# The seven block products in 26 up tiles of the MLP, with GpSimd forming the first of a pair's three weight sums instead of VectorE

## The chip, the cores and the metric

The kernel runs on one NeuronCore of a Trainium2 chip. The metric is the time of one execution on the device, in microseconds (us). Engines: TensorE (PE; PEld is its weight load), VectorE (DVE), ScalarE (ACT), GpSimd (POOL) and SyncE (SP), which here only issues transfers.

## The reference, cut to what matters

A Mamba-2 layer, shared keys and values, a differential attention layer, and then a second block: a mixer layer and an MLP, 512 tokens by 1024 features in fp32. The change touches the MLP, which is computed after 16 further tokens have been put in front (they are dropped again at the end):

```python
u = _rmsnorm(h, mlp_norm_g[l])
h = h + jnp.square(jax.nn.relu(u @ w_up[l])) @ w_down[l]   # w_up 1024 x 4096, w_down 4096 x 1024
h = _rmsnorm(h, final_norm_g)
```

## The kernel before

**Layout.** Activations are kept transposed: features on the 128 partitions, tokens along the free axis. An "up tile" is 128 of the 4096 columns of w_up for all 512 tokens: 8 blocks of 128x128 weights (a unit), each multiplied with 128 features x 512 tokens. Each fp32 product is made of three fp32r matmuls, high x high, high x low and low x high part, so a tile has 24 matmuls of 512 columns (`tile_of`, L522, matmul L543). The high part of a unit's weights is a copy by ScalarE (`hi`, L1143), the low part a subtraction by VectorE (`lo`, L1677: w_lo = w_raw - w_hi). w_raw, w_hi and w_lo have two slots each, a unit being loaded 512 KB at a time by SP's queue (`load`, L363), as soon as the low part of the unit before the last has been formed.

**The MLP.** 16 up tiles, 16 units of w_down over the features these gave (added to h), 16 more up tiles, and a last stage with the rest of w_down that puts out tokens on partitions (`down`, L1105). After an up tile VectorE takes relu(x) times the RMS norm's factor rt of each token from PSUM into ft (L2437), squares it (L2442) and subtracts (L2444), ScalarE squares it into b_hi (L1621); b_hi and b_lo are the high and low part for w_down. The norm's factor comes out of the first tiles' time: ScalarE's root, VectorE's reciprocal (L2430), a spread by TensorE, a copy into rt (L1614). In the last stage VectorE turns h into osb block by block (L2476) between the units.

**What sets the order.** Nothing is scheduled by a planner: each engine has its own list of instructions, written out by hand, and goes through it in order; waits on counting semaphores (raw, hi_ready, lo_ready, unit_done, acc_read, fh_ready, fl_ready) tie the lists together. An engine whose next instruction waits runs nothing of what stands behind it. GpSimd has nothing to do in the MLP but one transfer near its end (L515). Earlier in the kernel it makes two additions a group: L493 and L487 (one input there is a broadcast).

## Time and profile before

| | |
|---|---|
| median of 3 runs | 1231.15 us (1231.12 to 1231.21) |
| the profiled execution | span 1229.6 us, first to last instruction |
| TensorE busy | 1218.7 us (99%), 6181 matmuls |
| VectorE, ScalarE, GpSimd busy | 867.6 (71%), 596.6 (49%), 52.0 us (4%) |
| MLP's up and down tiles | 865.41 to 1133.65 us of the span |
| data moved | 115.24 MB, mean 94 GB/s |

The profile has this one execution; the median is over runs without it. A matmul's duration includes its way through the array, so durations of successive ones overlap; what a matmul costs is the distance between two starts. A group of rows has a busy time and the mean duration of one instruction; a timeline row has the start and the duration. What an engine idles ahead of an instruction stands in square brackets, with what ended it.

### The profile page before, as it was taken

Reading aid. Unit: us, or ns where it says so; the run is one execution under the profiler, and the core shown is the slowest. Engines: PE = TensorE matmul, PEld = TensorE weight load, DVE = VectorE, ACT = ScalarE, POOL = GpSimd, SP = SyncE. Lnnn points to the kernel's source line nnn. Section 1 sums busy time; section 2 is a strip of 40 time slices with the busy share of each in tenths; the row PEclk is TensorE's granted clock in tenths of the full one; section 3 lists DMA queues with packets and bytes.
Section 4 is the critical chain, followed back from the end, with each engine's and each line's share of the span. In section 5 each row is a group of like instructions: output and inputs, shape, how many; then the busy total and the mean of one; then the engine's idle time right before and its main releaser. Section 6 shows DMA issues by size and latency. Waiting matters only on the chain.

```text
span 1229.6 us, 17316 instructions
## 1 busy us (share of the span) xinstructions
PE 1218.7 (99%) x6181; PEld 990.3 (81%) x6181; DVE 867.6 (71%) x1342; ACT 596.6 (49%) x955; POOL 52.0 (4%) x46
## 2 busy tenths in 40 slices
PE   8999999999999999999999999999999999999997
PEld 6788888888888887878787899758888888888886
DVE  5888889888965366767777789997555332555676
ACT  6666755675653255565555553774323121222222
POOL 1010111111110000000000000000000000000000
PEclk9999999999999999999999999999999999999999
DMA  6433333333324322222222222124233323232322
GB/s 171 139 97 110 97 95 106 112 91 98 108 63 145 103 86 69 77 79 68 68 68 82 73 87 86 34 74 115 86 98 89 102 86 102 86 102 87 119 86 102
DMA packets 182606, 115.24 MB, mean 94 GB/s; under 512 B 3601, under 2 KB 175921, under 8 KB 181537
## 3 DMA queue, kind: packets, MB, share of 16 engines
q1 hardware_dynamic: 180672, 104.02, 29.1%
q0 software_dynamic: 1888, 10.62, 2.5%
q8 instruction: 28, 0.46, 0.2%
q14 instruction: 18, 0.14, 0.0%
HBM read 112.46 MB, written 2.16 MB: 93 GB/s over the span
## 4 chain that ended last, share of the span: by engine, by line
PE 96%; DVE 2%; DMA 1%; issue 0%; ACT 0%; SPq 0%; ACTq 0%
PE psum L543 66%; PE psum L1105 6%; PE psum L811 4%; PE psum L743 4%; PE psum L917 3%; PE psum L972 2%; PE psum L780 2%; PE psum L798 1%; PE psum L647 1%; PE psum L655 1%; PE psum L638 1%; PE psum L792 1%; PE psum L629 1%; PE psum L623 1%; PE psum L986 1%; PE psum L1056 1%
## 5 line engine op out<-in xcount | busy, mean ns | idle before, releaser
L1143 ACT ACTIVATE w_hi<-w_raw 128x1024 fp32r<-128x1024 f32 x184 | 194.4, 1057 | 412.2 <-PE psum L543 334.1
L1677 DVE TENSOR_TENSOR w_lo<-w_raw,w_hi 128x1024 fp32r<-128x1024 f32 x184 | 224.9, 1222 | 131.9 <-ACT w_hi L1143 131.5
L543 PE MATMUL psum<-a_hi,w_hi 128*128 128x512 f32 (+1 forms) x864 | 315.1, 380 | 0.2
L543 PE MATMUL psum<-a_lo,w_hi 128*128 128x512 f32 (+1 forms) x864 | 310.9, 375 | 0.0
L543 PE MATMUL psum<-a_hi,w_lo 128*128 128x512 f32 (+1 forms) x864 | 309.6, 373 | 0.0
L543 PEld LDWEIGHTS psum<-a_hi,w_hi 128*128 128x128 f32 x864 | 157.4, 188 | 34.2 <-issue 3.9
L543 PEld LDWEIGHTS psum<-a_hi,w_lo 128*128 128x128 f32 x864 | 157.2, 188 | 30.2
L543 PEld LDWEIGHTS psum<-a_lo,w_hi 128*128 128x128 f32 x864 | 157.0, 188 | 28.8
L543 PE MATMUL psum<-b_hi,w_hi 128*128 128x512 f32 x376 | 149.9, 399 | 0.0
L543 PE MATMUL psum<-b_lo,w_hi 128*128 128x512 f32 x376 | 148.6, 395 | 0.0
L543 PE MATMUL psum<-b_hi,w_lo 128*128 128x512 f32 x376 | 148.0, 394 | 0.0
L543 PEld LDWEIGHTS psum<-b_hi,w_hi 128*128 128x128 f32 x376 | 70.7, 188 | 21.8 <-issue 5.8
L543 PEld LDWEIGHTS psum<-b_hi,w_lo 128*128 128x128 f32 x376 | 70.7, 188 | 16.1
L543 PEld LDWEIGHTS psum<-b_lo,w_hi 128*128 128x128 f32 x376 | 70.6, 188 | 15.9 <-issue 0.2
L2437 DVE SCALAR_TENSOR_TENSOR arena<-psum,rt 128x512 f32<-128x512 f32 x32 | 22.1, 692 | 54.4 <-PE psum L543 52.5
L1105 PE MATMUL psum<-w_lo,b_hi 128*128 128x512 f32 x128 | 50.5, 394 | 0.0
L1105 PE MATMUL psum<-w_hi,b_lo 128*128 128x512 f32 x128 | 50.4, 394 | 0.0
L1105 PE MATMUL psum<-w_hi,b_hi 128*128 128x512 f32 x128 | 50.4, 394 | 0.0
L2228 DVE SCALAR_TENSOR_TENSOR arena<-arena,par 128x512 f32<-128x512 f32 x60 | 43.4, 750 | 0.6
L2476 DVE STREAM_TRANSPOSE arena<-h 32x128 f32<-32x128 f32 (+1 forms) x128 | 36.6, 286 | 3.9
L811 PE MATMUL psum<-w_hi,a_hi 128*128 128x256 f32 x128 | 36.8, 287 | 0.0
L811 PE MATMUL psum<-w_lo,a_hi 128*128 128x256 f32 x128 | 36.0, 281 | 0.0
(331 smaller groups left out, 1819.4 us busy)
## 6 DMA issues: line engine op xcount, KB each, us to landing
w_raw<-a_w_in SPq DMA_DIRECT2D x48, 512.0 KB, 3.8
w_raw<-w_up SPq DMA_DIRECT2D x32, 512.0 KB, 4.0
w_raw<-w_down SPq DMA_DIRECT2D x32, 512.0 KB, 3.8
arena<-acs POOLq DMA_DIRECT2D x8, 1024.0 KB, 5.0
w_raw<-a_w_out SPq DMA_DIRECT2D x16, 512.0 KB, 3.7
w_raw<-w_kv SPq DMA_DIRECT2D x16, 512.0 KB, 3.6
w_raw<-b_w_in SPq DMA_DIRECT2D x16, 512.0 KB, 3.8
w_raw<-w_in SPq DMA_DIRECT2D x14, 512.0 KB, 3.7
```

Of the source, the lines that this page charges most:

```text
L543: ins = mm(out, wv[:, u.par, k, :], xv[:, k0 + k, c0:c0 + cn], start=(first and begin and i == 0 and n == 0), stop=(last and end and i == ...
L743: ins = mm(bank((1, 0, 2, 3)[j]), wv[:, u.par, n, :], xv[:, k * KT + n, 0:SEQ], start=(k == 0 and n == 0 and i == 0), stop=(k == 1 and n = ...
L780: ins = mm(bank(2 + 2 * (q % 2) + i)[:, 0:P * (q + 1)], aq[64 * i:64 * i + 64, s.par, P * q:P * q + P], ak[64 * i:64 * i + 64, s.par, 0:P ...
L811: ins = mm(out, xv[:, 4 * part + k, P * c:P * c + P], value_block(wv, u)[:, k, :], start=(part == 0 and c % 2 == 0 and k == 0 and n == 0), ...
L917: ins = mm(acc(m), wv[:, u.par, 2 * k + j, :], xv[:, x, 0:SEQ], start=(k == 0 and n == 0), stop=(k == 3 and n == 2), skip_group_check=True)
L972: ins = mm(bank(2 * m.par), w_raw[:, u.par, k, :], h[:, k, META:T2], start=(k == 0), stop=(k == KT - 1), skip_group_check=True)
L1105: ins = mm(bank(4 * (1 - f) + i), b[:, k0 + k, P * i:P * i + P], w[:, k, :], start=(k0 + k == 0 and w is wh and b is b_hi and (f, i) != (1 ...
L1143: ac(w_hi[:, u.par, :, :], w_raw[:, u.par, :, :], ACT.Copy).then_inc(S["hi_ready"], 1)
L1677: tt(w_lo[:, u.par, :, :], w_raw[:, u.par, :, :], f32(w_hi[:, u.par, :, :]), ALU.subtract).then_inc(S["lo_ready"], 1)
L2228: ins = stt(dwo[:, j, :], src, par[:, at:at + 1], dwo[:, j, :], ALU.mult, ALU.add)
L2437: stt(ft, acc(m + (M_MLP + 24 * half)), 0.0, rt[:, 0:SEQ], ALU.max, ALU.mult).then_inc(S["acc_read"], 1)
L2476: own(nc.vector.transpose(osb[32 * q:32 * q + 32, 0:n, P * m + 32 * i:P * m + 32 * i + 32], h[32 * i:32 * i + 32, m, META:META + P * n].re ...
```

## The change

The 6 first up tiles stay as they are but for their tail: relu and square are now ScalarE's, without the factor rt. The factor is applied after w_down instead (its square on the sums, by VectorE; in the last stage with a per-token scalar, for which the residual is brought in scaled where it needs to be). The other 26 tiles go in 13 pairs, 5 in the first half and 8 in the second. A pair's product is seen as 2x2 blocks, [2 halves of the 1024 features] x [2 tiles] for the weights and [2 halves of the features] x [2 halves of the tokens] for the activations, and formed with seven block products instead of eight (Winograd's form of Strassen's scheme). Each block product has 4 blocks of 128 features, three matmuls each, and 256 tokens: 12 matmuls of 256 columns.

It needs sums on both sides. On the activations' side four (t1 to t4) are formed once, during the six plain tiles, by VectorE and ScalarE, high and low parts too. On the weights' side three for each pair: PR (two block sums in one addition, 1024 elements per partition), Q = one of PR's plus a block, U = Q plus a block (512 each). GpSimd forms PR (`pair_sum`), VectorE Q and U. High parts (A, D, PR, Q, U) are ScalarE's, low parts VectorE's. On the products' side ScalarE copies M1, U2 and M5 out of PSUM (`keep`), VectorE adds C22 and C12, ScalarE takes the relus of all four quarters and squares. Weights of a pair are loaded in one transfer of 1 MB (`load_pair`), into one of two places, once the low part D of the pair before the last is there; the place of even pairs lies over t3 and t4's fp32 form. The order of TensorE is M1, M4 of the pair before, M6, M2, M5, M7, M3.

Not shown: reading helpers that turn a name and a pair number into a semaphore and a count; `slot_free` (a high part waits for the product that last read its place); `keep`, `first_row`, `second_row`, `right_columns`, `squares_high`, `squares` (one ScalarE instruction each: copies of M1, U2, M5; relu of C11, of C21, of C12 and C22; the square into b_hi, the square in place); `pair_lo`, `b_pair`, `t_low` (one subtraction each); the list of both engines during the plain tiles; the last stage's added scalars.

```diff
+UP_PLAIN = 6
+U_DOWN = U_MLP + UP_PLAIN
+U_LAST = U_DOWN + 16
+U_END = U_LAST + 16
+PAIRS = (5, 8)
+PAIR0 = (0, 5)
...
+            def load_pair(q):
+                i = q - PAIR0[q >= PAIR0[1]]
+                src = t["w_up_2"].rearrange("(k p) m -> p k m", p=P)
+                c0 = P * (UP_PLAIN + 2 * q if q < PAIR0[1] else 16 + 2 * i)
+                sp.dma_start(pair_raw[i % 2].rearrange("p k a m -> p k (a m)"), src[:, :, c0:c0 + 2 * P]
+                             ).then_inc(on_raw(q)[0], 16)
+            def load_pairs(half, first, second):
+                for i in range(PAIRS[half]):
+                    q = PAIR0[half] + i
+                    if i < 2:
+                        sp.wait_ge(*(first, second)[i])
+                    else:
+                        sp.wait_ge(*on_lo("D", q - 2))
+                    load_pair(q)
+            for m in range(UP_PLAIN):
+                load(Lin(U_MLP + m), t["w_up_2"], 0, Lin(m * P))
+            load_pairs(0, (S["t_sum"], USED + T_DONE), (S["lo_ready"], U_DOWN))
...
+            load_pairs(1, on_lo("D", 4), (S["lo_ready"], U_LAST))
...
+            def pair_sum(q):
+                v = raw_of(q)
+                pool.wait_ge(*on_raw(q))
+                if q:
+                    pool.wait_ge(*on_lo("PR", q - 1))
+                else:
+                    pool.wait_ge(S["t_sum"], USED + T_DONE)
+                nc.gpsimd.tensor_tensor(sum_pr, v[:, 0], v[:, :, :, 1, :].rearrange("p h k m -> p k h m"), ALU.add
+                                        ).then_inc(S["w_sum"], 1)
+            for q in range(PAIR0[1] + PAIRS[1]):
+                pair_sum(q)
...
+            def product(name, q, wh, wl, xh, xl, out, first):
+                for k in range(4):
+                    for i, (wv, xv) in enumerate(((wh, xh), (wh, xl), (wl, xh))):
+                        ins = mm(out, wv[:, k, :], xv[:, k, :], start=(first and k == 0 and i == 0),
+                                 stop=(k == 3 and i == 2), skip_group_check=True)
+                ins.then_inc(on_pe(name, q)[0], 1)
...
+            def m4(q):
+                pe.wait_ge(*on_added("C22", q))
+                pe.wait_ge(*on_lo("D", q))
+                product("M4", q, s_hi["D"], s_lo["D"], t_hi[3], t_lo[3], pair_a(q), False)
+            def pairs(half):
+                for i in range(PAIRS[half]):
+                    q = PAIR0[half] + i
+                    m1(q)
+                    if i:
+                        m4(q - 1)
+                    if q == 0:
+                        pe.wait_ge(S["t_sum"], USED + T_DONE)
+                    pe.wait_ge(*on_kept("M1", q))
+                    product("M6", q, s_hi["Q"], s_lo["Q"], t_hi[1], t_lo[1], pair_a(q), False)
+                    product("M2", q, s_hi["A"][:, 1], s_lo["A"][:, 1], x_block(a_hi, 1, 0), x_block(a_lo, 1, 0),
+                            bank(1)[:, 0:256], False)
+                    pe.wait_ge(*on_lo("PR", q))
+                    if i:
+                        pe.wait_ge(*on_added("C12", q - 1))
+                    else:
+                        pe.wait_ge(S["acc_read"], M_DOWN + 8 * half)
+                    if q == 0:
+                        pe.wait_ge(S["t_sum"], USED + T_DONE + 1)
+                    product("M5", q, s_hi["PR"][:, :, 1], s_lo["PR"][:, :, 1], t_hi[0], t_lo[0], bank(0)[:, 0:256], True)
+                    pe.wait_ge(*on_kept("U2", q))
+                    product("M7", q, s_hi["PR"][:, :, 0], s_lo["PR"][:, :, 0], t_hi[2], t_lo[2], pair_a(q), False)
+                    pe.wait_ge(*on_lo("U", q))
+                    pe.wait_ge(*on_kept("M5", q))
+                    product("M3", q, s_hi["U"], s_lo["U"], x_block(a_hi, 1, 1), x_block(a_lo, 1, 1),
+                            bank(0)[:, 0:256], False)
+                m4(q)
...
+            def up(m):
+                act.wait_ge(S["unit_done"], U_MLP + m + 1)
+                if m >= 2:
+                    act.wait_ge(S["fl_ready"], m - 1)
+                v = fts[0][:, m % 2, :]
+                ac(v, acc(Lin(M_MLP + m)), ACT.Relu).then_inc(S["acc_read"], 1)
+                act.wait_ge(S["acc_read"], M_MLP + m + 1)
+                ac(b_hi[:, m, 0:SEQ], v, ACT.Square)
+                ac(v, v, ACT.Square).then_inc(S["fh_ready"], 1)
...
+            def pair_hi(name, q):
+                slot_free(name, q)
+                if name in ("A", "D"):
+                    act.wait_ge(*on_raw(q))
+                    src = raw_of(q)[:, :, :, 0, :] if name == "A" else raw_of(q)[:, 1, :, 1, :]
+                else:
+                    act.wait_ge(*on_sum(name, q))
+                    src = {"PR": sum_pr, "Q": sum_q, "U": sum_u}[name]
+                ac(s_hi[name], src, ACT.Copy).then_inc(on_hi(name, q)[0], 1)
...
+            def pairs(half):
+                n, q0 = PAIRS[half], PAIR0[half]
+                for i in range(n):
+                    q = q0 + i
+                    pair_hi("U", q)
+                    keep("M1", q)
+                    if i:
+                        second_row(q - 1)
+                    pair_hi("D", q)
+                    if i:
+                        right_columns(q - 1)
+                    keep("U2", q)
+                    if i < n - 1:
+                        pair_hi("Q", q + 1)
+                    if i:
+                        squares_high(q - 1)
+                    if i < n - 1:
+                        pair_hi("A", q + 1)
+                    keep("M5", q)
+                    if i:
+                        squares(q - 1)
+                    first_row(q)
+                    if i < n - 1:
+                        pair_hi("PR", q + 1)
+                u = (U_DOWN, U_LAST)[half]
+                act.wait_ge(*on_pe("M7", q))
+                hi(Lin(u))
+                right_columns(q)
+                second_row(q)
+                hi(Lin(u + 1))
+                squares_high(q)
+                squares(q)
+            ac(gfm[:, :], par[:, C_MLP:C_MLP + KT], ACT.Copy, scale=-1.0).then_inc(S["t_hi"], 1)
+            act.wait_ge(S["t_sum"], USED + 1)
+            for k in range(4):
+                ins = ac(t_f32[0][:, k, :], t_f32[0][:, k, :], ACT.Copy, scale=par[:, C_MLP + k:C_MLP + k + 1])
+            ins.then_inc(S["t_hi"], 1)
...
+            pair_hi("Q", 0)
+            pair_hi("A", 0)
+            up(4)
+            pair_hi("PR", 0)
+            act.wait_ge(S["half_read"], USED + 1)
+            ac(t_hi[0], t_f32[0], ACT.Copy).then_inc(S["t_hi"], 1)
+            up(5)
+            pairs(0)
...
+            def pair_sums(q, names):
+                v = raw_of(q)
+                for name in names:
+                    if q:
+                        dve.wait_ge(*on_lo(name, q - 1))
+                    if name == "Q":
+                        dve.wait_ge(*on_sum("PR", q))
+                        tt(sum_q, sum_pr[:, :, 1, :], v[:, 0, :, 0, :], ALU.add).then_inc(S["w_sum"], 1)
+                    else:
+                        dve.wait_ge(*on_sum("Q", q))
+                        tt(sum_u, sum_q, v[:, 1, :, 0, :], ALU.add).then_inc(S["w_sum"], 1)
...
+            def add_c22(q):
+                dve.wait_ge(*on_pe("M7", q))
+                dve.wait_ge(*on_kept("M5", q))
+                stt(fts[q % 2][:, 1, 256:512], bank(2 + q % 2)[:, 0:256], -1.0, keep_m5, ALU.mult, ALU.subtract
+                    ).then_inc(S["w_added"], 1)
+            def add_c12(q):
+                dve.wait_ge(*on_pe("M3", q))
+                tt(fts[q % 2][:, 0, 256:512], bank(0)[:, 0:256], keep_u2, ALU.add).then_inc(S["w_added"], 1)
...
+            def pairs(half):
+                n, q0 = PAIRS[half], PAIR0[half]
+                for i in range(n):
+                    q = q0 + i
+                    pair_lo("U", q)
+                    pair_lo("D", q)
+                    if i < n - 1:
+                        pair_sums(q + 1, ("Q", "U"))
+                        pair_lo("Q", q + 1)
+                        pair_lo("A", q + 1)
+                    if i:
+                        b_pair(q - 1)
+                    add_c22(q)
+                    if i < n - 1:
+                        pair_lo("PR", q + 1)
+                    add_c12(q)
+                u = (U_DOWN, U_LAST)[half]
+                lo(Lin(u))
+                lo(Lin(u + 1))
+                b_pair(q)
...
+            for m in range(8):
+                u = U_DOWN + 2 * m
+                if m < 7:
+                    lo(Lin(u + 2))
+                else:
+                    pair_sums(5, ("Q", "U"))
+                dve.wait_ge(S["unit_done"], u + 2)
+                part = fts[0][:, 0, :]
+                tt(part, acc(Lin(M_DOWN + m)), rt[:, 0:SEQ], ALU.mult).then_inc(S["acc_read"], 1)
+                dve.wait_ge(S["acc_read"], M_DOWN + m + 1)
+                own.mark(tt(h[:, m, META:T2], h[:, m, META:T2], part, ALU.add))
+                if m < 7:
+                    lo(Lin(u + 3))
+                else:
+                    pair_lo("Q", 5)
+                    pair_lo("A", 5)
+                    pair_lo("PR", 5)
+            pairs(1)
```

## Rows read from the trace of the kernel before

**Rows 1.** The page's chain of work that ended last, shares of the span by engine.

```profile
PE 96%; DVE 2%; DMA 1%; issue 0%; ACT 0%; SPq 0%; ACTq 0%
```

**Rows 2.** Busy time by stage: us from:to, length, then each engine's busy time (instructions), clock, DMA share, GB/s.

```profile
1038.00:1133.80 95.80, 95.80 (x415) 77.69 (x414) 51.32 (x63) 25.84 (x32) 0.00 (x0) 1.00 0.33 98
```

**Rows 3.** Timeline of TensorE: start us, duration us, engine line op out<-in.

```profile
900.13 0.39 PE L543 MATMUL psum<-a_hi,w_hi 128*128 128x512 f32 x1
...
955.73 0.39 PE L543 MATMUL psum<-b_hi,w_hi 128*128 128x512 f32 x1
...
1044.69 0.39 PE L543 MATMUL psum<-a_hi,w_hi 128*128 128x512 f32 x1
...
1133.65 0.39 PE L1105 MATMUL psum<-w_hi,b_hi 128*128 128x512 f32 x1
```

**Rows 4.** Timeline of TensorE in the attention layer, matmuls of 256 columns.

```profile
442.76 0.28 PE L811 MATMUL psum<-w_hi,a_lo 128*128 128x256 f32 x1
...
445.01 0.28 PE L811 MATMUL psum<-w_lo,a_hi 128*128 128x256 f32 x1
```

**Rows 5.** Groups by shape, whole kernel: busy us, mean ns | idle before, released by.

```profile
L1143 ACT ACTIVATE w_hi<-w_raw 128x1024 fp32r<-128x1024 f32 x184 | 194.4, 1057 | 412.2 <-PE psum L543 334.1 <-PE psum L1105 56.6 <-PE psum L743 13.4
...
L1388 ACT ACTIVATE arena<-psum 128x384 f32<-128x384 f32 x16 | 7.0, 487 | 30.4 <-PE psum L792 30.4
...
L1398 ACT ACTIVATE arena<-psum 128x128 f32<-128x128 f32 x32 | 8.4, 278 | 22.5 <-PE psum L798 22.5
...
L1677 DVE TENSOR_TENSOR w_lo<-w_raw,w_hi 128x1024 fp32r<-128x1024 f32 x184 | 224.9, 1222 | 131.9 <-ACT w_hi L1143 131.5
...
L1858 DVE TENSOR_TENSOR arena<-arena,psum 128x256 f32<-128x256 f32 x16 | 6.7, 421 | 0.6
```

**Rows 6.** Timeline of ScalarE and VectorE behind an up tile.

```profile
883.65 1.06 ACT L1143 ACTIVATE w_hi<-w_raw 128x1024 fp32r<-128x1024 f32 x1 [3.92 <-PE psum L543]
...
884.62 0.62 ACT L1621 ACTIVATE b_hi<-arena 128x512 f32 x1
...
884.75 1.23 DVE L1677 TENSOR_TENSOR w_lo<-w_raw,w_hi 128x1024 fp32r<-128x1024 f32 x1 [0.40 <-ACT w_hi L1143]
...
885.89 0.69 DVE L2442 TENSOR_TENSOR arena<-arena 128x512 f32<-128x512 f32 x1
```

**Rows 7.** Group of GpSimd's 2048-wide addition, one input broadcast.

```profile
L487 POOL TENSOR_TENSOR arena<-arena,gacs 128x2048 f32<-128x2048 f32 x7 | 25.6, 3651 | 0.6
```

**Rows 8.** Timeline around GpSimd's 512-wide additions, the first and the last of eight.

```profile
82.68 1.22 DVE L1677 TENSOR_TENSOR w_lo<-w_raw,w_hi 128x1024 fp32r<-128x1024 f32 x1
...
83.34 1.71 POOL L493 TENSOR_TENSOR arena<-arena 128x512 f32<-128x512 f32 x1 [13.46 <-ACT arena L1244]
...
84.00 1.61 DVE L1778 SCALAR_TENSOR_TENSOR arena<-arena,gconv 128x512 f32<-128x512 f32 x1
...
85.64 0.75 DVE L1779 SCALAR_TENSOR_TENSOR arena<-arena,gconv 128x512 f32<-128x512 f32 x1
...
362.75 1.30 POOL L493 TENSOR_TENSOR arena<-arena 128x512 f32<-128x512 f32 x1 [21.75 <-ACT arena L1244]
```

**Rows 9.** Timeline of VectorE during GpSimd's 2048-wide addition of 90.81 to 94.46.

```profile
92.42 0.69 DVE L1771 TENSOR_TENSOR arena<-psum,rt 128x512 f32<-128x512 f32 x1 [0.18 <-PE psum L543]
```

**Rows 10.** Timeline of the start of the MLP.

```profile
868.45 0.75 DVE L2416 SCALAR_TENSOR_TENSOR a_lo<-h,par,a_hi  x1
...
871.78 0.47 PE L543 MATMUL psum<-a_hi,w_hi 128*128 128x512 f32 x1
...
873.89 0.18 DVE L2430 RECIPROCAL stat<-stat 128x4 f32<-128x4 f32 x1 [0.35 <-ACT stat L1153]
```

**Rows 11.** Transfers by issue: queue, count, KB each, median us from issue to landing.

```profile
w_raw<-w_up SPq DMA_DIRECT2D x32, 512.0 KB, 4.0
...
w_raw<-b_w_out SPq DMA_DIRECT2D x8, 512.0 KB, 3.4
...
arena<-acs POOLq DMA_DIRECT2D x8, 1024.0 KB, 5.0
```

## What the change does to the time: the prediction

> **What bounds the kernel now.** I read the chain of work that ended last first: 96% of the span is TensorE [rows 1], so time goes only where its matmuls stop or become fewer. The stage table shows the same for the second half's up tiles: TensorE is busy for all of 95.80 us, VectorE for 51.32, ScalarE for 25.84 [rows 2]. The beat of TensorE is read from starts, not from durations, which overlap: 384 matmuls of 512 columns lie between 955.73 and 1044.69 and again between 1044.69 and 1133.65 [rows 3], 0.2317 us each, so a plain up tile (24 of them) takes 5.56 us and two take 11.12. For half as many columns, the 19 starts from 442.76 to 445.01 give 0.118 us [rows 4] although each has its own weight load: a narrow matmul costs half, and the weight loads stay hidden. The clock is at full speed all through this stage [rows 2].
>
> **What is removed: one product in eight.** A pair of tiles was 48 wide matmuls, 11.12 us. It becomes 7 x 4 x 3 = 84 narrow ones, 84 x 0.117 = 9.84 us, 1.41 a product. Were TensorE never to wait, 13 pairs would give 13 x 1.28 = 16.6 us.
>
> **What is added: work on the other engines.** Per pair ScalarE gets two 1024-wide and three 512-wide high parts, five 256-wide copies or Relus, one 512-wide Relu and two 1024-wide squares. A 1024-wide one takes 1.06 us [rows 5], but in a row the next one starts 0.97 after it, and a 512-wide one counts 0.53 (0.62 less that overlap) [rows 6]. For 256 elements out of PSUM I take 0.38, between 0.28 for 128 and 0.49 for 384 [rows 5], 0.29 in a row. Sum: 4 x 0.97 + 4 x 0.53 + 5 x 0.29 = 7.5 us. VectorE gets three 1024-wide (1.23 [rows 5], 1.15 in a row [rows 6]), five 512-wide (0.69, 0.61 in a row) and two 256-wide ones (0.42 [rows 5], 0.34 in a row): 7.2 us. Both fit into 9.84. So it is not the load that decides, it is the order.
>
> **The price of GpSimd's sum.** No row has this add: 1024 elements from two SBUF inputs. The nearest: 512 elements took 1.30 us with VectorE quiet [rows 8], 2048 with one broadcast input 3.65 [rows 7]. The line through these gives 2.08, doubling the first 2.60. I take 2.35, the middle; both ends are kept.
> The Trainium skill (GPSIMD Engine Reference, § 3.1) has a two-input add of 2048 fp32 elements at 4497 ns; half of it, 2.25, is an estimate that would make the period below 10.7 and the kernel 1229.5 us; no run here shows that size. Its § 4.1 sends elementwise adds to VectorE, which speaks against this change.
> The second part of the price is in VectorE's rows: a two-input operation that started at 84.00, while GpSimd's add of 83.34 to 85.05 ran, took 1.61 us [rows 8] where the same ones take 0.75 otherwise; it ended 0.56 after GpSimd did. GpSimd in turn took 1.71 instead of 1.30, with a VectorE subtraction in flight at its start [rows 8]. An operation with one input in PSUM kept its 0.69 beside GpSimd's 2048-wide add [rows 9]. So one of the two with two SBUF inputs waits for the other, and all of VectorE's sums and low parts have two.
>
> **The chain that sets a pair's time.** After pair_lo("PR") VectorE has add_c12, lo U, lo D, then sum Q, which waits for GpSimd's sum, which waits for that same lo PR. From its end: handoff 0.08, GpSimd 2.35; lo U, held until then, ends 0.50 later (0.69 less the 0.19 by which the held one was shorter); lo D 0.61; sum Q 0.61; handoff 0.04 (884.71 to 884.75 [rows 6]); on ScalarE hi Q 0.53, squares_high 0.97, hi A 0.97, keep M5 0.29, squares 1.06; handoff 0.04; on VectorE b_pair 1.15, add_c22 0.34, the next lo PR 1.22. Sum 10.76 us. If lo U gets in ahead of GpSimd, it is 10.87. I take 10.8 a pair. TensorE, with 9.84, would wait some 0.9 us, before M3, which needs keep M5 (its end at 7.0 of the period, while M7 is done at 6.3). M4 then comes at once, since C22 is there when M1 has run. The other cycle (M4, second_row, hi D, lo D) has hi D 1 us before lo D can start, so it doesn't count.
>
> **The start of the MLP.** VectorE is free at 869.2 [rows 10] and now has, before its reciprocal: the first difference 1.2, a wait for ScalarE's four scalings 1.6, four 256-wide steps 1.6, lo 1.2. The reciprocal ends at about 875.0 instead of 874.07 [rows 10]; TensorE has done half of tile 1 (started at 871.78 [rows 10]) at 874.6, so it waits 0.4 us and the plain tiles end at 900.5 instead of 900.13 [rows 3].
>
> **The first pairs.** load_pair(0) waits for t_low(4), since its buffer holds t3 and t4. ScalarE and VectorE work through their lists behind tile 2's end, so t_low(4) ends at about 889.1. A load is now 1 MB. Those of 512 KB took 3.4 to 4.0 us, the lower number being that of b_w_out's, which reads runs of 1 KB as these do; 1024 KB of acs took 5.0 [rows 11]. Bounds 5.0 and 8.0 (twice 4.0); I take 5.0, since the one row with this size has it: landed 894.2. Then GpSimd 2.4 and sum Q 0.7: 897.4. ScalarE follows with hi Q 0.53, hi A 0.97, up(4) 1.75, hi PR 0.97, t_hi 0.97, up(5) 1.75, hi U 0.53, keep M1 0.38: 905.3. M1(0) runs at 900.5, M6(0) at 905.4: TensorE waits 3.4 us there. M3(0) starts at 911.05, lo PR(1) ends at 913.6. Three periods, 32.4, bring 946.0 for lo PR(4). The last pair has no next one to prepare: M4(3) ends 0.6 after that, five products 7.05, M4(4) waits 0.3 for squares(3), b_pair(3) and add_c22(4), then 1.4: 955.5. Before, the down tiles started at 955.73 [rows 3]: -0.2 us for the first half, where 5 x 1.28 = 6.4 were on offer.
>
> **The down tiles** keep their 88.96 us. VectorE has two operations more a tile instead of one (0.7 + 0.7 where it had 0.7, beside two low parts of 1.23, in 11.1 us of TensorE); that is covered. Without the cover it would cost 8 x 0.7.
>
> **The second pairs.** VectorE's last h addition stands ahead of lo Q(5) and lo A(5), and waits for all down tiles. From the end of down: 0.2 + 0.69 + 0.04 + 0.69 + 0.04, lo Q 0.61, lo A 1.22 = 3.5 us in which TensorE stands; M6(5) waits 0.7 more for keep M1(5). lo PR(6) ends 13.9 after the end of down. Six periods 64.8, the last pair 9.55 as above: 88.25 instead of 88.96, -0.7 us.
>
> **The last stage** keeps its matmuls; the residual additions are one operation each as before, one tiny one and a 512-wide one more: +0.1.
>
> **Sum.** -0.2 - 0.7 + 0.1 = -0.8 us. The profiled execution has a span of 1229.6 us and the median of the runs is 1231.15, so 1.55 us lie around the span: 1228.8 + 1.55 = 1230.4 us. This kernel's measurement can tell about 0.2%, 2.5 us, from no change.
>
> **Rivals.**
> (a) GpSimd's sum doesn't hold VectorE (other buffers, other moment). Then lo U and lo D run beside it, sum Q ends 3.12 after lo PR instead of 4.15, the chain is 9.73 and TensorE's 9.84 bounds. Nine periods by 0.9: 1222.3 us. Against it: the 1.61 [rows 8]. Chance 0.15.
> (b) Slower: GpSimd's sum is longer than my bound, or has to wait for VectorE's next operation also. Each us goes into the chain nine times and into both starts. From 2.65 on the kernel is slower than before by anything one can measure; at 3.0 the period is 11.4, the time 1230.4 + 9 x 0.6 = 1236. Chance 0.2.
> (c) Slower: the loads. load_pair(q) leaves after lo D(q-2), 3.5 us after lo PR; the sum needs it 10.8 + 0.1 after that lo PR, so 7.3 us may pass. At the bound of 8.0 the first load is 3.0 us later, once, and each period 0.7 longer: 1230.4 + 3.0 + 9 x 0.7 = 1239.7; from 7.6 on the kernel is measurably slower. For it: a load moves twice the bytes; against it: the 5.0 [rows 11]. Chance 0.1.
> My forecast has 0.55, with a range of its own from 1228 (sum at 2.08) to 1233 (sum at 2.60 and load at 5.6).
>
> **How the numbers follow.** Faster by over 0.2% (below 1228.7): (a) and 0.13 of the forecast's 0.55, 0.28. Slower (over 1233.6): (b) and (c) without their mild part, 0.27, and 0.06 for starts longer than worked out, 0.33. Between: 0.39. The range takes in (a) and most of (b) and (c): 1222.5 to 1238.
>
> **What would show it.** In the profile after: a distance of 10.8 us from one M3 to the next, not 9.84 or 11.1; TensorE idle about 0.9 us ahead of each M3, released by ScalarE's copy into keep_m5; 13 GpSimd adds of 2.1 to 2.6 us, and VectorE's subtraction for U with 2 us instead of 0.69; gaps of 3.4 us after M1(0) and of 3.5 us ahead of M1(5). The prediction is wrong if TensorE waits ahead of another product, if GpSimd waits for a DMA, or if the period is TensorE's own.

## The result, and the profile after

| | before | after |
|---|---|---|
| median (lowest to highest) of 15 runs | 1231.11 us (1230.72 to 1232.94) | 1236.88 us (1233.16 to 1239.13) |
| profiled execution, span | 1229.6 us | 1235.6 us |
| TensorE busy | 1218.7 us | 1212.1 us |

The ratio is 1.0041, 95% interval 1.0033 to 1.0049: the change makes the kernel 5.8 us slower. The forecast was 1230.4 us, no change that could be measured. The time lies in the range, but on the slow side, which had a chance of 0.33, and it got there by a mechanism that none of the rivals named: the range held by luck. The 15 runs don't scatter at random. The two with a mean granted clock of 0.999 took 1233.16 and 1233.27 us, those with 0.994 or 0.995 took 1236.5 to 1237.3. A mean of 0.999 leaves room for at most 3.7 us at half clock in the whole run, its end included (estimate: 2 x 0.0015 x 1231.6), where the profiled run has 10.2 us at the two starts that are described below.

The page of the kernel after: engines, then of the picture in 40 slices the rows of TensorE and its clock, the chain of work that ended last, and the new load.

```profile
PE 1212.1 (98%) x6649; PEld 1007.6 (82%) x6649; DVE 912.7 (74%) x1386; ACT 668.2 (54%) x1093; POOL 84.3 (7%) x59
...
PE   9999999999999999999999999999989999999997
...
PEclk9999999999999999999999999999989999999999
...
PE 85%; DVE 8%; ACT 3%; issue 2%; DMA 2%; POOL 0%; SPq 0%; ACTq 0%; DVEq 0%
...
arena<-w_up SPq DMA_DIRECT2D x7, 1024.0 KB, 5.3
```

TensorE's part of the chain fell from 96% [rows 1] to 85%, VectorE's rose from 2% to 8%. The single 8 in each row of the picture is the slice in which the first pairs start, and it is in the clock's row too: TensorE not only waited there, it ran slower afterwards. The stage table of after shows it (from:to, length, then busy time of TensorE, its weight loads, VectorE, ScalarE and GpSimd, granted clock, DMA share, GB/s):

```profile
905.00:909.00 4.00, 3.15 (x15) 3.19 (x16) 4.00 (x4) 1.47 (x4) 1.91 (x1) 0.50 0.00 0
912.00:959.00 47.00, 45.24 (x379) 44.69 (x378) 35.98 (x40) 32.06 (x55) 7.20 (x3) 1.00 0.25 78
959.40:1048.40 89.00, 89.00 (x385) 71.93 (x384) 32.10 (x35) 20.83 (x21) 2.40 (x1) 1.00 0.36 106
...
1052.00:1055.00 3.00, 2.89 (x12) 2.59 (x12) 1.58 (x2) 0.08 (x1) 1.88 (x1) 0.50 0.00 0
1056.00:1139.00 83.00, 78.93 (x657) 77.85 (x657) 67.45 (x74) 56.63 (x96) 14.40 (x6) 1.00 0.28 90
```

The clock was at half (1.2 GHz instead of 2.4) behind the start of the first pairs and behind the start of the second, and full in between; before had 1.00 in its up and down tiles, as in [rows 2]. The records put the two stretches at 904.99, for 6.83 us, and at 1051.76, for 3.41 us. The matmuls show the same (TensorE's timeline of after at the two starts):

```profile
902.60 0.28 PE L1196 MATMUL psum<-a_hi,pair_lo 128*128 128x256 f32 x1
905.85 0.55 PE L1196 MATMUL psum<-t_hi,q_hi 128*128 128x256 f32 x1 [2.97 <-ACT psum L1841]
906.19 0.42 PE L1196 MATMUL psum<-t_lo,q_hi 128*128 128x256 f32 x1
...
935.06 0.35 PE L1196 MATMUL psum<-a_hi,w_hi 128*128 128x256 f32 x1 [0.75 <-ACT arena L1841]
...
945.98 0.36 PE L1196 MATMUL psum<-a_hi,w_hi 128*128 128x256 f32 x1 [0.76 <-ACT arena L1841]
...
1048.13 0.40 PE L663 MATMUL psum<-b_hi,w_lo 128*128 128x512 f32 x1
1051.99 0.55 PE L1196 MATMUL psum<-a_hi,pair_hi 128*128 128x256 f32 x1 [3.46 <-DVE pair_lo L2760]
1052.34 0.41 PE L1196 MATMUL psum<-a_lo,pair_hi 128*128 128x256 f32 x1
...
1055.35 0.39 PE L1196 MATMUL psum<-t_hi,q_hi 128*128 128x256 f32 x1 [0.46 <-ACT psum L1841]
```

Behind a pause of 3.25 us (902.60 to 905.85; pauses here are always from start to start) and of 3.86 us (1048.13 to 1051.99) a 256-column matmul takes 0.21 us instead of 0.118 [rows 4]. The small pauses ahead of each M3, released by ScalarE's copy into keep_m5 (L1841), leave the clock up. The distance from M3 to M3 is 945.98 - 935.06 = 10.92 us; 10.8 was forecast. Only seven of the 13 M3 have this pause; between the first two pairs of each half, and into the last one, the distance is 9.94 to 10.02 us.

What the distance is made of, in the timeline of VectorE, GpSimd and ScalarE for pair 2 of after:

```profile
926.50 1.22 DVE L2760 TENSOR_TENSOR w_lo<-arena,w_hi 128x1024 fp32r<-128x1024 f32 x1
927.63 0.42 DVE L2782 TENSOR_TENSOR arena<-psum,mixw 128x256 f32<-128x256 f32 x1
927.86 2.41 POOL L629 TENSOR_TENSOR arena<-w_raw 128x1024 f32<-128x1024 f32 x1 [8.53 <-DVE w_lo L2760]
927.96 2.85 DVE L2760 TENSOR_TENSOR w_lo<-mixw,w_hi 128x512 fp32r<-128x512 f32 x1
...
930.73 0.68 DVE L2760 TENSOR_TENSOR w_lo<-arena,w_hi 128x512 fp32r<-128x512 f32 x1
931.34 0.68 DVE L2750 TENSOR_TENSOR arena<-arena,w_raw 128x512 f32<-128x512 f32 x1
...
928.95 0.62 ACT L1820 ACTIVATE w_hi<-arena 128x512 fp32r<-128x512 f32 x1
...
932.11 0.64 ACT L1820 ACTIVATE q_hi<-arena 128x512 fp32r<-128x512 f32 x1 [1.57 <-DVE arena L2750]
...
932.65 1.05 ACT L1869 ACTIVATE b_hi<-arena 128x1024 fp32r<-128x1024 f32 x1
...
933.60 1.04 ACT L1820 ACTIVATE pair_hi<-w_raw 128x1024 fp32r<-128x1024 f32 x1
934.55 0.36 ACT L1841 ACTIVATE arena<-psum 128x256 f32<-128x256 f32 x1
```

These are the steps in the forecast's order: lo PR, add_c12, GpSimd's sum, and beside it lo U, which takes 2.85 us instead of 0.69 and ends at 930.81, 0.54 after GpSimd; then lo D, sum Q, hi Q, the square, hi A, keep M5. The row of 928.95 is hi D. Over all 13 pairs (groups by shape, MLP's stretch: busy us, mean ns | idle before; GpSimd's sum has two groups because a pair's weights have two places):

```profile
L629 POOL TENSOR_TENSOR arena<-arena 128x1024 f32<-128x1024 f32 x7 | 16.8, 2397 | 658.1 <-DMA arena<-w_up 614.5 <-DVE w_lo L2760 43.6
L629 POOL TENSOR_TENSOR arena<-w_raw 128x1024 f32<-128x1024 f32 x6 | 15.5, 2582 | 55.0 <-DVE w_lo L2760 55.0
...
L2760 DVE TENSOR_TENSOR w_lo<-mixw,w_hi 128x512 fp32r<-128x512 f32 x13 | 28.3, 2177 | 0.0
```

The mean of 2582 ns hides something. Eleven of the 13 sums took 2.39 to 2.41 us. Pair 1's took 3.21 and pair 6's 2.68, each having started while a subtraction of VectorE with two inputs was running. TensorE waited for neither of them. The longest:

```profile
903.71 3.21 POOL L629 TENSOR_TENSOR arena<-w_raw 128x1024 f32<-128x1024 f32 x1 [6.37 <-DVE w_lo L2760]
```

The hold costs VectorE 1.5 us a pair on average: lo U takes 2.8 us or more in nine pairs and 0.69 or less in the four in which it starts while no sum of GpSimd is running. The Trainium skill (SBUF — State Buffer, § Who interferes with whom) says that VectorE with two inputs in SBUF and GpSimd reading SBUF exclude each other through a shared read port. The trace agrees: the subtraction was held until GpSimd had ended, and GpSimd's sum was the longer one where the subtraction had started first. ScalarE's row of 928.95, beside both, keeps its 0.62 us [rows 6].

**Where the time went.** Segment by segment against the forecast, from the starts in the two traces:

| segment | forecast | measured | difference |
|---|---|---|---|
| start of the kernel to M6(0), with its 3.4 us pause | 905.4 | 905.85 | +0.45 |
| M6(0) to M3(0) | 5.65 | 8.42 | +2.8 |
| M3(0) to the down tiles | 44.45 | 45.07 | +0.6 |
| down tiles | 88.96 | 89.02 | +0.1 |
| end of down to M3(5) | 11.25 | 12.79 | +1.5 |
| M3(5) to the last stage | 77.0 | 77.89 | +0.9 |
| last stage | 96.0 | 96.5 | +0.5 |

Together 6.8 us: the span was to shrink by 0.8 and grew by 6.0. Behind M6(0), 28 matmuls at 0.213 instead of 0.118 are 2.7 us; behind M1(5), 12 of them and the slow restart are 1.3. That is 4.0 us for the clock, and 0.8 for the period (seven periods by 0.12). The rest, 2.0 us, is spread over terms that were each 0.1 to 0.5 too small; no experiment took them apart.

### The profile page after: what moved, and what is told of

Same layout as the page of the kernel before. It is cut to its first block, busy times and chain, and to the rows that moved or that the text cites. A ratio compares the mean times of both kernels' runs of the same rounds, so it can differ in the third digit from the quotient of the medians.

```text
span 1235.6 us, 18052 instructions
## 1 busy us (share of the span) xinstructions
PE 1212.1 (98%) x6649; PEld 1007.6 (82%) x6649; DVE 912.7 (74%) x1386; ACT 668.2 (54%) x1093; POOL 84.3 (7%) x59
## 4 chain that ended last, share of the span: by engine, by line
PE 85%; DVE 8%; ACT 3%; issue 2%; DMA 2%; POOL 0%; SPq 0%; ACTq 0%; DVEq 0%
PE psum L663 52%; PE psum L1285 6%; PE psum L933 4%; PE psum L865 4%; DVE w_lo L2760 3%; PE psum L1196 3%; PE psum L1039 3%; PE psum L1094 2%; PE psum L902 2%; PE psum L920 1%; PE psum L769 1%; PE psum L777 1%; PE psum L760 1%; DVE pair_lo L2760 1%; ACT b_hi L1869 1%
## 5 line engine op out<-in xcount | busy, mean ns | idle before, releaser
L1321 ACT ACTIVATE w_hi<-w_raw 128x1024 fp32r<-128x1024 f32 x158 | 166.8, 1056 | 279.7 <-PE psum L663 203.8
L1991 DVE TENSOR_TENSOR w_lo<-w_raw,w_hi 128x1024 fp32r<-128x1024 f32 x158 | 193.0, 1222 | 111.2 <-ACT w_hi L1321 110.6
L663 PE MATMUL psum<-a_hi,w_hi 128*128 128x512 f32 (+1 forms) x656 | 233.4, 376 | 0.2
L663 PE MATMUL psum<-a_lo,w_hi 128*128 128x512 f32 (+1 forms) x656 | 228.7, 368 | 0.0
L663 PE MATMUL psum<-a_hi,w_lo 128*128 128x512 f32 (+1 forms) x656 | 227.9, 367 | 0.0
L663 PEld LDWEIGHTS psum<-a_hi,w_hi 128*128 128x128 f32 x656 | 118.3, 188 | 24.7 <-issue 3.9
L663 PEld LDWEIGHTS psum<-a_hi,w_lo 128*128 128x128 f32 x656 | 118.1, 188 | 21.4
L663 PEld LDWEIGHTS psum<-a_lo,w_hi 128*128 128x128 f32 x656 | 118.0, 188 | 19.7
L629 POOL TENSOR_TENSOR arena<-arena 128x1024 f32<-128x1024 f32 x7 | 16.8, 2397 | 658.1 <-DMA arena<-w_up 614.5
```

The costliest lines, as they stand in the source:

```text
L663: ins = mm(out, wv[:, u.par, k, :], xv[:, k0 + k, c0:c0 + cn], start=(first and begin and i == 0 and n == 0), stop=(last and end and i == ...
L1321: ac(w_hi[:, u.par, :, :], w_raw[:, u.par, :, :], ACT.Copy).then_inc(S["hi_ready"], 1)
L1991: tt(w_lo[:, u.par, :, :], w_raw[:, u.par, :, :], f32(w_hi[:, u.par, :, :]), ALU.subtract).then_inc(S["lo_ready"], 1)
```

## The experiments

**Theory.** (T1) The two pauses at the starts are long enough for TensorE to lose its clock, and this costs 4 us on top of the waits. (T2) The period of 10.92 us comes from the order of VectorE's list: sum Q, on which TensorE depends through hi Q and keep M5, stands behind lo U, which GpSimd holds, and behind lo D. Rivals: the clock fell for another reason, or its fall is only a sign of the wait; and the period is due to GpSimd itself (its 2.4 us and the hold), so that it goes when VectorE forms PR. The kernel before, run beside the experiments, took 1230.93, 1231.09 and 1231.19 us.

**e5_before_held: a pause put into the kernel before.** There are no pairs in it, so a fall of the clock can only come from the pause. ScalarE makes two copies behind the last down tile, and TensorE waits for them. They change nothing in the output.

```diff
+                if half == 1:
+                    pe.wait_ge(S["warm_set"], 2)
...
+                if half == 1:
+                    act.wait_ge(S["unit_done"], U_MLP + 32)
+                    ac(scratch, osb[:, :, 0:SEQ], ACT.Copy)
+                    ac(osb[:, :, SEQ:D], osb[:, :, 0:SEQ], ACT.Copy).then_inc(S["warm_set"], 1)
```

> The kernel before with one thing more: ahead of the second half's first up tile TensorE waits for two 2048-wide copies of ScalarE that nobody needs, a hold of about 3.9 us in the middle of work at full clock. Theory of the clock: a single idle stretch of this length is enough, the granted clock then stands at 0.5 for 3.4 to 6.8 us, in which the plain tiles lose half their pace: 1231.0 + 3.9 + (1.7 to 3.4) = 1236.6 to 1238.3 us. Rival: the clock fell in the changed kernel for another reason (its narrow matmuls, two idle stretches in each pair): then only the hold is paid, 1234.9 us, and no stretch at 0.5 is seen there.

Measured: 1238.19 us (1237.61 to 1239.13), ratio 1.006 (1.0043 to 1.0077), +7.1 us. TensorE's timeline around the pause, and the stage table of the eight matmuls behind it:

```profile
1043.96 0.40 PE L543 MATMUL psum<-b_hi,w_lo 128*128 128x512 f32 x1
1049.37 0.79 PE L543 MATMUL psum<-a_hi,w_hi 128*128 128x512 f32 x1 [5.01 <-ACT arena L1635]
1049.96 0.63 PE L543 MATMUL psum<-a_lo,w_hi 128*128 128x512 f32 x1
1050.39 0.63 PE L543 MATMUL psum<-a_hi,w_lo 128*128 128x512 f32 x1
...
1052.87 0.39 PE L543 MATMUL psum<-a_hi,w_lo 128*128 128x512 f32 x1
```

```profile
1049.35:1052.70 3.35, 3.33 (x8) 2.66 (x9) 0.00 (x0) 0.00 (x0) 0.00 (x0) 0.50 0.22 66
```

The pause was 5.4 us, longer than meant, so the total doesn't judge between the expectations. The rows do: eight matmuls 0.43 us apart where they are 0.23 apart otherwise, at a granted clock of 0.50, and the 384 matmuls from 1049.37 took 90.61 us instead of the 88.96 of before. A pause alone, without pairs, GpSimd or a changed list, brings the fall, and the fall costs 1.65 us for 3.41 us at half clock.

**e1_filler: the pauses filled.** 25 matmuls of 256 columns behind M1(0) and 30 behind the down tiles, into a bank that nothing reads. Nothing is left out.

```diff
+            def filler(n):
+                for _ in range(n):
+                    mm(bank(5)[:, 0:256], a_hi[:, 0, 0:P], a_hi[:, 0, 0:256], start=True, stop=True,
+                       skip_group_check=True)
...
+                        filler(25)
...
+            filler(30)
```

> Theory: the changed kernel's loss of more than its pair periods comes from TensorE's two long gaps (3.25 us ahead of M6(0), 3.86 us ahead of M1(5)), after which the granted clock stands at 0.5 for 6.8 and 3.4 us and M6 and M2 of the first pair and M1 of the sixth take 2.6 us each instead of 1.4. Filling the gaps with 25 and 30 matmuls of 256 columns, whose results nobody reads, leaves all waits as they are and keeps the clock: no stretch at 0.5 before the end, M3(0) about 2.9 us earlier, the time 4.1 us lower: 1232.8 us. Rival: the slow products cost nothing, since ScalarE and VectorE set the pace there too, or the fall of the clock doesn't come from the gap: the time stays at 1236.9 us, with the clock or without it.

Measured: 1233.39 us (1232.91 to 1235.01), ratio 1.0019 (1.0009 to 1.0028), 3.5 us less than after. The same waits are there, and the stage table has the clock at full through both starts (the fillers count as TensorE's work):

```profile
905.00:909.00 4.00, 3.99 (x34) 3.82 (x33) 3.75 (x3) 2.85 (x6) 3.25 (x1) 1.00 0.00 0
...
1049.80:1055.00 5.20, 4.74 (x39) 4.49 (x38) 4.16 (x4) 1.11 (x3) 2.69 (x1) 1.00 0.00 0
```

Useless work made the kernel faster, so what it saved was the clock. Together with e5 this settles T1, and it gives the price, 3.5 us of the 5.8. The two runs of after with a mean clock of 0.999 took the same 1233.2 us without fillers. The profiled run of e1 has one fall of its own, at 9.07 us for 3.41 us, in the first stage and far from the fillers; it took 1.6 us more than the median.

**e2_vector_sum: VectorE forms PR, GpSimd does nothing.** In the same list, ahead of sum Q.

```diff
-            for q in range(PAIR0[1] + PAIRS[1]):
-                pair_sum(q)
...
+                    if name == "PR":
+                        dve.wait_ge(*on_raw(q))
+                        tt(sum_pr, v[:, 0], v[:, :, :, 1, :].rearrange("p h k m -> p k h m"), ALU.add
+                           ).then_inc(S["w_sum"], 1)
...
-                        pair_sums(q + 1, ("Q", "U"))
+                        pair_sums(q + 1, ("PR", "Q", "U"))
...
```

(the same for the first pair of each half.)

> The part of the change that names GpSimd, undone: VectorE forms PR ahead of Q, behind the low part D. Theory A: in this order of VectorE's list the period is also held by the cycle M4, second_row, hi D, lo D, (sum PR 1.15), sum Q, hi Q, two 1024-wide steps, hi A, keep M5, M3, M1, M4: 5.05 + 2.84 + 0.12 + 2.91 = 10.92 us, as long as with GpSimd. The period stays at 10.9, GpSimd's hold on lo U (2.18 us) goes without a gain, and the time is within 1.5 us of 1236.9 (the first sum is some 1.1 us faster, so rather 1236). Rival B: GpSimd's addition and its hold on lo U are the whole price of the period: without them the chain is 9.9 us, and the time 7 x 1.0 us lower, 1229.9 us.

Measured: 1238.32 us (1237.36 to 1239.88), ratio 1.0064 (1.0047 to 1.0081), 1.4 us more than after. The timeline of VectorE in a pair of the second half, and of TensorE at its M3:

```profile
1074.36 0.68 DVE L2762 TENSOR_TENSOR w_lo<-mixw,w_hi 128x512 fp32r<-128x512 f32 x1
1075.98 0.69 DVE L2762 TENSOR_TENSOR w_lo<-arena,w_hi 128x512 fp32r<-128x512 f32 x1 [0.94 <-ACT w_hi L1818]
1076.59 1.22 DVE L2748 TENSOR_TENSOR arena<-w_raw 128x1024 f32<-128x1024 f32 x1
```

```profile
1070.51 0.36 PE L1194 MATMUL psum<-a_hi,w_hi 128*128 128x256 f32 x1 [0.96 <-ACT arena L1839]
...
1081.64 0.35 PE L1194 MATMUL psum<-a_hi,w_hi 128*128 128x256 f32 x1 [0.96 <-ACT arena L1839]
```

lo U is back at 0.68 us, GpSimd is out of it, and the period is 11.13 us, longer than with GpSimd. Now VectorE stands for 0.94 us ahead of lo D, waiting for ScalarE's hi D. That is the cycle which the prediction had put aside ("so it doesn't count"): M4, second_row, hi D, lo D, sum Q, hi Q, keep M5, M3, and from there M4 again. The cycle had indeed room in after (lo D starts at 930.73, 1.2 us behind hi D's end at 929.57); with PR between lo D and sum Q it is 1.3 us longer (1076.59 to 1077.91, the start of sum Q) and becomes the bound: 10.92 - 1.2 + 1.3 = 11.0 of the 11.13 us. So the period doesn't go when GpSimd's sum goes: T2's rival has fallen. The expectation had 10.92 us, 0.2 too little.

**e3_q_first and e8_q_first_d: sum Q moved up.** GpSimd forms PR as in after. Only VectorE's list is changed: sum Q first, then lo U, sum U, lo D (e3), or lo U, lo D, sum U (e8).

```diff
                     q = q0 + i
+                    if i < n - 1:
+                        pair_sums(q + 1, ("Q",))
                     pair_lo("U", q)
                     pair_lo("D", q)
                     if i < n - 1:
-                        pair_sums(q + 1, ("Q", "U"))
+                        pair_sums(q + 1, ("U",))
                         pair_lo("Q", q + 1)
```

(the edit of e8; in e3 the sum U stands ahead of lo D.)

> GpSimd keeps PR; only VectorE's list is put in another order: sum Q, lo U, sum U, lo D instead of lo U, lo D, sum Q, sum U. Theory: what holds the period at 10.92 us is that sum Q stands behind lo U and lo D; from the end of lo PR to the end of sum Q it is 4.3 us, now 0.14 + 2.41 + 0.04 + 0.69 = 3.3. The chain is 9.9 us, TensorE's own 9.85 nearly bounds, the gap ahead of each M3 goes: 7 x 1.0 us less, 1229.6 us, the two gaps at the starts and the slow clock behind them stay. Rival: the load on VectorE and GpSimd, not the order, sets the period: it stays above 10.6 and the time above 1234.

> As the run with sum Q first, but with lo D ahead of sum U. In that run the period was 9.93 for four pairs and then 10.5, and GpSimd waited for the weights' transfer: lo D, transfer 5.3, GpSimd 2.4, sum Q 0.69, lo U, sum U, lo D make 10.5. Theory: the transfer chain is next in line; lo D 0.65 earlier brings it to 9.8, below TensorE's 9.85, the gaps ahead of M3 fall below 0.2 us and the time is 3 us lower: 1228.1 us. Rival: the transfer isn't the cause, GpSimd's addition just falls onto more of VectorE's work: the period stays at 10.5 and the time within 1 us of 1231.1.

Measured for e3: 1231.13 us (1230.54 to 1232.46), ratio 1.0002 (0.9993 to 1.0012). Its period is 9.93 us at first (M6 at 1063.39, 1073.32, 1083.25) and then 10.1, 10.6, 10.5. Queue and engines in a late pair of e3:

```profile
1098.54 0.37 SPq L530 DMA_DIRECT2D arena<-w_up  x1
...
1103.87 2.39 POOL L629 TENSOR_TENSOR arena<-arena 128x1024 f32<-128x1024 f32 x1 [8.08 <-DMA arena<-w_up]
1106.36 0.69 DVE L2750 TENSOR_TENSOR arena<-arena 128x512 f32<-128x512 f32 x1 [2.81 <-POOL arena L629]
```

GpSimd now waits for the load, not for lo PR. This is the prediction's rival (c), which didn't happen in after and was next in line: lo D frees the load's place, the load takes 5.3 us, GpSimd 2.4, then VectorE has four operations to the next lo D, 10.5 in all. The sum U ahead of lo D made the load late by 0.6 each time.

Measured for e8: 1228.76 us (1227.18 to 1232.55), ratio 0.9981 (0.9971 to 0.9991), 8.1 less than after. Timeline of e8, two pairs' M6, then GpSimd and VectorE between them:

```profile
1082.14 0.28 PE L1196 MATMUL psum<-t_hi,q_hi 128*128 128x256 f32 x1
...
1092.08 0.28 PE L1196 MATMUL psum<-t_hi,q_hi 128*128 128x256 f32 x1
```

```profile
1090.94 2.40 POOL L629 TENSOR_TENSOR arena<-w_raw 128x1024 f32<-128x1024 f32 x1 [7.58 <-DVE w_lo L2760]
...
1093.45 0.69 DVE L2750 TENSOR_TENSOR arena<-arena,w_raw 128x512 f32<-128x512 f32 x1 [2.31 <-POOL arena L629]
```

From the second M6 of each half on the distance is 9.93 or 9.94 us, TensorE's own (84 matmuls by 0.118), and TensorE waits ahead of no product there. GpSimd's 2.40 us are unchanged, and VectorE even stands still for 2.31 us beside them. T2 holds: with GpSimd's sum left as it was, the order of the list gave the 1 us a pair back, in the seven pairs that had lost it. What isn't shown is how much of this is the hold and how much the place of sum Q: with sum Q first, VectorE waits while GpSimd's sum runs, so the edit removes both, and the hold alone (rival (a)) was not tested. The clock still fell at both starts of the profiled run, for 3.41 us each. In after it was 6.83 at the first, so of the 8.1 us between the two profiled runs 7.0 lie in the periods and 1.1 in this shorter fall.

**e4_low_early: the second start.** lo Q, lo A and lo PR of pair 5 stand ahead of VectorE's wait for the last down tile instead of behind it.

```diff
                     pair_sums(5, ("Q", "U"))
+                    pair_lo("Q", 5)
+                    pair_lo("A", 5)
+                    pair_lo("PR", 5)
                 dve.wait_ge(S["unit_done"], u + 2)
...
-                else:
-                    pair_lo("Q", 5)
-                    pair_lo("A", 5)
-                    pair_lo("PR", 5)
```

> Only the low parts Q, A and PR of pair 5 are moved ahead of VectorE's wait for the last unit of the down tiles. Theory: the gap of 3.86 us ahead of M1(5) goes, and with it the 3.4 us at half clock that cost 1.3 us: 1236.9 - 3.6 - 1.3 = 1232.0 us, one stretch at 0.5 left (behind M1(0)). Rival: the start of the second pairs is given back, because the chain of ScalarE and VectorE sets the end of the half anyway: under 2 us gained.

Measured: 1231.13 us (1228.88 to 1232.41), ratio 0.9998 (0.9989 to 1.0008), 5.8 less than after. The pause of 3.86 us ahead of M1(5) is gone, and so is the fall behind it, as the stage table shows; 0.73 us, start to start, ahead of M6(5) are left. The other fall, 6.83 us from 904.89, is still there.

```profile
1049.80:1055.00 5.20, 4.74 (x40) 4.60 (x39) 3.90 (x7) 2.89 (x6) 0.00 (x0) 1.00 0.42 124
```

**All together, with either engine.** e6: order of e8, e4's edit and 25 fillers behind M1(0), GpSimd forms PR. e7: the same with VectorE forming PR ahead of sum Q, 17 fillers. e10 and e9: e6 and e7 without fillers.

> All three remedies at once, GpSimd still forming PR: sum Q first with lo D ahead of sum U, the low parts of pair 5 early, 25 filler matmuls in the gap behind M1(0). If the losses are separate they add up: 1228.1 (with the order alone) - 5.7 (low parts early, as measured) - 2.9 (clock behind M1(0)) = 1219.5 us, no stretch at half clock before the end. If they overlap, something between 1222 and 1226 us.

> The same with VectorE forming PR, directly ahead of sum Q; 17 fillers, since the gap is shorter then. VectorE has 8.4 us of work a pair, below 9.85. Theory: once the order is right, who forms PR is of little weight in the period; the first sum comes 1.2 us earlier and no operation is held: 1218.5 us, 0 to 2 us below the run with GpSimd. Rival: VectorE's added 1.15 us stands in the chain (sum PR, sum Q, hi Q) and the period rises above 10.3: over 1223 us.

> The run with all three remedies and GpSimd's sum, without the 25 fillers: the gap behind M1(0) is 3.3 us again, idle. Theory of the clock: a stretch of 3.4 or 6.8 us at half clock behind it in most executions, that is 1.5 to 2.9 us more than the 1222.5 us with fillers: 1224.0 to 1225.4 us. Rival: with the order mended the chain has the room to take the slow products in: 1222.5 us.

> The run with all three remedies and VectorE's sum, without the 17 fillers. The idle gap behind M1(0) is 2.3 us then. In the run with VectorE's sum in the old order the clock stood after a gap of 2.36 us and fell after one of 3.86. Theory: 2.3 us of idling don't cost the clock, the time is that with fillers, 1220.7 us. Rival: any gap of a few us does it: 1222.2 to 1223.6 us.

| kernel | PR formed by | fillers | median us | ratio (95%) |
|---|---|---|---|---|
| e6 | GpSimd | 25 | 1222.49 (1222.3 to 1222.71) | 0.993 (0.9914 to 0.9947) |
| e7 | VectorE | 17 | 1220.68 (1220.6 to 1222.57) | 0.992 (0.9903 to 0.9936) |
| e10 | GpSimd | none | 1224.32 (1223.08 to 1224.96) | 0.9941 (0.9924 to 0.9958) |
| e9 | VectorE | none | 1221.07 (1220.5 to 1221.82) | 0.9919 (0.9902 to 0.9935) |

The stage table of e10 and of e9 at the first start, and of e9 in the second pairs, and the M6(0) of each:

```profile
907.00:911.00 4.00, 4.00 (x23) 4.00 (x23) 4.00 (x6) 0.95 (x3) 0.71 (x1) 0.59 0.00 0
```

```profile
906.64 0.36 PE L1196 MATMUL psum<-t_hi,q_hi 128*128 128x256 f32 x1 [2.96 <-ACT psum L1841]
```

```profile
903.00:907.00 4.00, 2.38 (x20) 2.41 (x21) 3.64 (x6) 2.70 (x7) 0.00 (x0) 1.00 0.00 0
1056.00:1120.00 64.00, 64.00 (x544) 64.00 (x543) 49.66 (x65) 49.46 (x84) 0.00 (x0) 1.00 0.32 97
```

```profile
904.62 0.36 PE L1194 MATMUL psum<-t_hi,q_hi 128*128 128x256 f32 x1 [2.15 <-ACT psum L1839]
```

In the pairs TensorE is busy for 64.00 of 64.00 us. With GpSimd in the first start's chain the pause is 3.25 us (2.96 in the row) and the clock fell at 907.71 for 3.41 us; with VectorE it is 2.43 and the clock stayed. So the fillers are worth 1.8 us to the one (1224.32 - 1222.49) and 0.4, within the spread, to the other. Without fillers VectorE is ahead by 3.3 us, with them by 1.8: e7's M6(0) starts 1.1 us earlier than e6's (904.33 and 905.45), and this lead is the same in the second half (M6(5) at 1044.22 and 1045.34), so 1.1 us come from the first chain, where nothing hides the longer sum; the rest was not followed. The periods are equal. e6 lies 3.0 us above what the sum of the single gains gives (3.5 + 5.8 + 8.1), and e7 missed its 1218.5 by 2.2. The gains overlap: the fall behind the second start, 1.3 us, is in e1's and in e4's, and the shorter fall at the first, 1.1 us by the profiled runs, in e1's and in e8's. 0.6 us weren't located.

e9 beats both kernels, by 0.8% against before, without fillers. It is the new scheme with two remedies, and GpSimd forms nothing in it.

## Why the prediction went wrong, point by point

- **The engines' loads, "not the load, it is the order"**: right. VectorE at 67 of 83 us and ScalarE at 57 had room, and the same operations in e8's order reach TensorE's own beat.
- **The price of GpSimd's sum**, 2.35 us between 2.08 and 2.60: measured 2.40 in eleven pairs, 3.21 and 2.68 in two. **The hold on VectorE** (rival (a) says there is none): right, 0.54 us between the ends where 0.50 was worked out. That e6 comes near rival (a)'s 1222.3 is chance: e6 has another order, early low parts and fillers, where rival (a) has only the hold gone.
- **The chain of a pair**: right in each member and its sequence; 10.92 instead of 10.8 us, as lo PR's end to sum Q's end took 4.30 instead of 4.15. Apart from the starts TensorE made no pause of over 0.55 us, start to start, but those ahead of M3, 0.75 us in the rows' brackets and 0.91 by the starts (1.03 - 0.118), where "some 0.9" was named. It did so in seven pairs, not in nine. The second cycle, through hi D, doesn't count in after, as was said; it does in e2.
- **A pair of 9.84 us of TensorE's**: 9.93. The prediction's own row gave 0.118 a matmul [rows 4], and its sum took 0.117. Small here.
- **The two starts**: M6(0) at 905.4 was 905.85, M1(5) 3.5 us late was 3.86 from start to start (3.46 in the row). The waits were right, and this is the step that failed: they were charged at their length ("TensorE waits 3.4 us there", "3.5 us in which TensorE stands"). The price of a wait on TensorE has a second term, the matmuls behind it at half clock. It was 2.7 and 1.3 us here, 4.0 of the 6.8 us by which the span missed the forecast. Without them (e1) the kernel is at 1233.4, still 3.0 us above the forecast and slower than before, by the period and the small terms of the table. The prediction had read the clock of before as 1.00 [rows 2] and took it as given. Before has no pause of TensorE of this length in the MLP, and its longest anywhere, 2.44 us at 6.57, left the clock up. So the clock behind 3.4 us of waiting was unknown and should have stood in the sum as such. The nearest place that was kept for it is the 0.06 for "starts longer than worked out". The Trainium skill (TensorE: Matmul & The Clock Gate, § HAM oscillation — how this bites in real kernels) has this case: pauses between bursts of matmuls that throw the clock back, again and again. The traces agree for 3.86 and 5.41 us, with 0.50 behind each; behind 3.25 us it was so in four of five profiled runs.
- **Rivals**: (b), a longer GpSimd sum, and (c), the loads, were slower cases with other causes. (b)'s second cause, GpSimd's sum waiting for VectorE, did happen, in the sums of 3.21 and 2.68 us, but not in a pair whose M3 waited. (c) decides from 7.3 us of landing, the landing was 5.3, and it came true only where the order was changed (e3), at 10.5 us a pair.
- **The last stage** at +0.1 was +0.6, not followed further.

## What to carry to other kernels

Price a new wait of the bottleneck engine twice: its length, and what the clock does behind it. Before a smaller amount of work on TensorE is counted as a gain, look where it now has to wait. Then move the one operation on which it depends ahead of what nobody waits for yet. In a list worked through in order this counted for more than which engine does the step: 8.1 us by moving one sum. The choice between GpSimd and VectorE was worth 1.4 us for GpSimd in the old order, and in the new one 1.8 us for VectorE, or 3.3 without fillers, where the clock came on top.

## What the runs showed of the hardware that was not expected

- In the profiled runs the clock fell behind MLP pauses of 3.25 (after, e4, e8, e10), 3.86 (after, e2, e3, e8) and 5.41 us (e5) and stayed up behind pauses of 1.03 (after, seven M3), 2.36 (e2) and 2.43 us (e9). In e3's profiled run it also stayed up behind one of 3.25 (2.97 us in the row, as in after), so at that length it goes either way from run to run. The two runs of after at 0.999 must have kept it behind at least one of their pauses, and by their time, 1233.2 us as with fillers, probably behind both.
- The length of the pause alone doesn't decide. In the kernel's first stage, where TensorE has only short bursts, the clock fell at 9.07 us in e1, behind a pause of 2.29 us (6.63 to 8.92), and stayed up behind 2.44 us in before.
- The runs of after spread over 1233 to 1239 us, and their mean clock over 0.999 to 0.993. That the clock's falls make this spread is likely, but only one of the runs has a trace.
- In the MLP it stayed at half for 3.41 or for 6.83 us. A part of it can lie in the pause itself: in after it fell at 904.99, and TensorE began again at 905.85. 3.41 us cost 1.65 us of matmuls (e5).
- A matmul of 256 columns takes 0.213 us at half clock and 0.118 at full, of 512 columns 0.43 and 0.23. The weight load of each (188 ns) doesn't show at either width.
- Held behind GpSimd's 1024-element sum, VectorE's 512-element subtraction took up to 2.85 us and ended 0.54 us after it. Started behind VectorE's 1024-element subtraction (903.48 to 904.70), GpSimd's sum took 3.21 us instead of 2.40.
